# Two transformer blocks on one core: the opening by passes, top-k rounds paced by issued tiles, and a gate product between short latent products

## What is computed

```python
def reference(x, ...):
    x = first_block(x, ...)    # pooling, gated linear attention (GLA), forgetting attention (fox), feed-forward
    x = second_block(x, ...)
    return x

def second_block(x, ...):                                  # D = 1024, T = 512
    h = rmsnorm(x)
    (q_lat, c_kv, k_rope, z_a, q_b, k_b, v_b, z_b,
     q_idx, k_idx, w_idx, gate_a, gate_b) = split(h @ w_in)
    # latent attention (mla): 8 heads, queries from a latent of 384, keys and values from one of 256
    q = rmsnorm(q_lat) @ w_uq;   k, v_a = rmsnorm(c_kv) @ w_ukv       # rope on 32 of 96 features
    y_a = softmax(mask(q @ k)) @ v_a * silu(z_a)
    # sparse attention (dsa): 8 heads; an index score picks the keys of each query
    score = sum_heads(relu(q_idx @ k_idx) * w_idx);  idx = top_k(score, 128)
    y_b = softmax(q_b @ k_b[idx] + rel_bias) @ v_b[idx] * silu(z_b)
    x = x + (sigmoid(gate_a) * (y_a @ w_o_a) + sigmoid(gate_b) * (y_b @ w_o_b)) @ w_out
    return rmsnorm(x)
```

## Time and profile before

| | before |
|---|---|
| three runs | 1049.06, 1048.12, 1049.0 us; median 1049.0 |
| profiled execution | 1049.3 us, of which the span of its trace is 1047.5 us |
| mean granted clock of TensorE | 0.997 |
| busy: PE, PEld, DVE, ACT, POOL | 98%, 79%, 58%, 42%, 31% |
| matmuls | 5126 |
| dense tiles (form HH, WH of line 1454) | 800 matmuls, 403 ns each |
| moved by DMA | 102.39 MB, mean 98 GB/s |

### The profile page before, as it was taken

How to read it: one execution, slowest core, us unless ns; L and a number is a source line. 1 busy time by engine, 2 the same in 40 slices (tenths; PEclk the granted TensorE clock), 3 DMA queues, 4 the chain that set the end, 5 groups by cost and what they waited for, 6 DMA issues and landing times.

```text
span 1047.5 us, 13717 instructions
## 1 busy us (share of the span) xinstructions
PE 1030.2 (98%) x5126; PEld 832.4 (79%) x5126; DVE 603.8 (58%) x1087; ACT 443.9 (42%) x785; POOL 320.5 (31%) x374
## 2 busy tenths in 40 slices
PE   9999999999999999999999999989999999999997
PEld 7887877778888888888888878767887777788886
DVE  5875657575444432444457657888656666335544
ACT  6432656554232221233242346445755554323233
POOL 1344632440110000110113347333336666521101
PEclk9999999999999999999999999999999999999999
DMA  8222233123323322323322335211322323222312
GB/s 287 92 71 86 82 91 94 62 77 104 100 84 104 115 92 90 101 81 101 101 101 89 126 115 190 81 61 45 98 67 85 116 88 109 84 98 95 106 61 81
DMA packets 34898, 102.39 MB, mean 98 GB/s; under 512 B 4608, under 2 KB 8128, under 8 KB 34832
## 3 DMA queue, kind: packets, MB, share of 16 engines
q1 hardware_dynamic: 34560, 101.25, 29.7%
q10 hardware_dynamic: 272, 0.26, 0.1%
HBM read 93.40 MB, written 4.74 MB: 94 GB/s over the span
## 4 chain that ended last, share of the span: by engine, by line
PE 85%; DVE 8%; ACT 3%; issue 2%; DMA 1%; POOL 0%; SPq 0%; DVEq 0%; ACTq 0%; POOLq 0%
PE bank L1454 23%; PE bank L1458 23%; PE bank L1456 23%; PE bank L1586 3%; PE bank L1577 2%; PE bank L1477 1%; DVE score L2147 1%; PE bank L1478 1%; PE bank L1479 1%; DVE m L2145 1%; PE bank L1562 1%; DVE acc L1875 1%; ACT WH L1638 1%; DMA X<-xT 1%; PE bank L1496 1%
## 5 line engine op out<-in xcount | busy, mean ns | idle before, releaser
L1454 PE MATMUL bank<-HH,WH 128*128 128x512 f32 x800 | 322.7, 403 | 0.9 <-DVE HL L1866 0.6
L1458 PE MATMUL bank<-HH,WL 128*128 128x512 f32 x800 | 312.9, 391 | 0.0
L1456 PE MATMUL bank<-HL,WH 128*128 128x512 f32 x800 | 312.5, 391 | 0.0
L2234 POOL TENSOR_TENSOR WL<-WS,WH 128x256 fp32r<-128x256 f32 x256 | 203.5, 795 | 255.6 <-ACT WH L1638 239.6
L1638 ACT ACTIVATE WH<-WS 128x1024 fp32r<-128x1024 f32 x160 | 166.3, 1047 | 41.6 <-PE bank L1458 40.2
L1454 PEld LDWEIGHTS bank<-HH,WH 128*128 128x128 f32 x800 | 151.0, 189 | 38.5 <-issue 5.8
L1458 PEld LDWEIGHTS bank<-HH,WL 128*128 128x128 f32 x800 | 150.4, 188 | 32.3
L1456 PEld LDWEIGHTS bank<-HL,WH 128*128 128x128 f32 x800 | 150.9, 189 | 29.4 <-issue 1.4
L1856 DVE TENSOR_TENSOR WL<-WS,WH 128x1024 fp32r<-128x1024 f32 x96 | 125.1, 1308 | 30.8 <-ACT WH L1638 30.8
L2275 POOL TENSOR_TENSOR fa<-fa,fg 128x512 f32<-128x512 f32 x22 | 28.3, 1286 | 271.6 <-DVE fa L2087 271.6
L1454 PE MATMUL bank<-GH,WH 128*128 128x512 f32 x176 | 68.5, 389 | 0.0
(11 more groups left out here) (326 smaller groups left out, 1710.7 us busy)
## 6 DMA issues: line engine op xcount, KB each, us to landing
WS<-wall SPq DMA_DIRECT2D x161, 512.0 KB, 3.4
scratch<-rows SPq DMA_DIRECT2D x8, 320.0 KB, 5.4
X<-xT SPq DMA_DIRECT2D x8, 256.0 KB, 6.8
b_t<-scratch SPq DMA_DIRECT2D x8, 256.0 KB, 3.6
outT<-X SPq DMA_DIRECT2D x7, 256.0 KB, 2.3
b_m<-b_m SPq DMA_DIRECT2D x11, 128.0 KB, 2.3
f_s<-f_s SPq DMA_DIRECT2D x8, 128.0 KB
f_m<-f_m SPq DMA_DIRECT2D x8, 128.0 KB
```

Of the source, the lines that this page charges most:

```text
L1454: e.matmul(b[:, :], wh, xh[:, at_k, :], start=k == 0, stop=False)
L1456: e.matmul(b[:, :], wh, xl[:, at_k, :], start=False, stop=False)
L1458: m = e.matmul(b[:, :], wl, xh[:, at_k, :], start=False, stop=k == n - 1)
L2234: e.tensor_tensor(WL[:, u % NW, cs], WS[:, u % NST, cs], f32(WH[:, u % NW, cs]), ALU.subtract).then_inc(*tick(w_low_g, u if c == 3 else (u ...
```

## The change

It has four parts.

1. *Opening.* 10 fillers in place of 14. Chunk 0 of `X` is loaded by a DMA that ACT issues as its first instruction, and not by SP; SP's order after it is `V`, first half of unit 0, chunk 1, second half, chunk 2, unit 1, chunks 3 and 4, unit 2. ACT splits chunk 0 before the first half of unit 0. A new step `mm_firsts` has the three products of a chunk go together by passes: three times HH x WH, then three times HL x WH, then three times HH x WL, each with its own wait.
2. *Latent products.* `uq0` takes a bank of `t_ring`. The product `za1` no longer follows `uq3`; it comes ahead of `uk1`, that is between `uq1` and `uk1`.
3. *Pace of the top-k rounds.* `now["per"]` is 0 here. A wrapper `paced` around `attention` adds 0.25 for each yield of attention and 0.37 for each tile issued since (2 for a token-side product), and issues a round (or a step of `dsa_stack`) for each whole unit.
4. *Mixes.* `attention` yields once more ahead of each mix of latent attention, so that one more dense step lies there.

```diff
@@ the opening
-        do("split_first", half=0)
         for c in range(NK):
             do("halve_x", c=c)
             known.add(("h1", c))
-            if c == 0:
-                do("split_first", half=1)
+            if c < 2:
+                do("split_first", half=c)
                 unit_low[0], count["split"] = w_low_v, 1
...
-            for (name, _, _, _), (t, _), b in zip(firsts, tiles, early):
-                do("mm", name=name, tiles=[(t, k)], n=NK, x="h1", x0=0, b=b, free=None)
+            do("mm_firsts", names=[f[0] for f in firsts], tiles=[t for t, _ in tiles], k=k, b=early)
@@ attention
                         if to_c:
+                            if to_c[0]["a"] == "mla":
+                                yield
                             step_c()
@@ mla_products
-                                   + cols(96 * hd + 64, 16), "lq", 3, q_out(hd, hl))
-            if p:
+                                   + cols(96 * hd + 64, 16), "lq", 3, q_out(hd, hl),
+                                   ring=t_ring if hd == 0 else d_ring)
+            if p > 1:
                 yield from z_products("za", P_ZA, p)
@@ mla_side
+            yield from z_products("za", P_ZA, 1)
             yield from mla_products(1)
@@ the weave of the second block's attention
-        now["per"] = 1.5
+        def paced(main, per_tile, per_step):
+
+            due, seen = 0.0, len(steps)
+            for _ in main:
+                yield
+                due += per_step + per_tile * sum(len(s["tiles"]) if kind == "mm" else 2 * (kind == "mm_tok")
+                                                 for kind, s in steps[seen:])
+                seen = len(steps)
+                while due >= 1:
+                    due -= 1
+                    step_behind()
+
+        now["per"] = 0.0
...
+        weave(paced(attention(...), .37, .25), side, [0.9] * 66 + [0.85])
@@ SP
-                    for c in range(NK):
+                    for c in range(1, NK):
                         e.dma_start(X[:, c, :], xT[:, c, :]).then_inc(*x_in[c].tick())
-                        if c == 0:
+                        if c == 1:
                             e.dma_start(WS[:, 0, 512:1024], wall[0, :, 512:1024]).then_inc(*w_in[0].tick(0))
-                        elif c in (1, 3):
-                            load((c + 1) // 2)
+                        elif c in (2, 4):
+                            load(c // 2)
@@ TensorE
-                    for _ in range(14):
+                    for _ in range(10):
                         e.matmul(bank[2][:, 0:128], ones[:, :], ones[:, :], start=True, stop=True)
...
+                elif kind == "mm_firsts":
+
+                    k = s["k"]
+                    for t, b in zip(s["tiles"], s["b"]):
+                        q.wait_ge(hi(("h1", k)), w_hi("first" if t < 4 else t // UT))
+                        e.matmul(b[:, :], weights(t)[0], HH[:, k, :], start=k == 0, stop=False)
+                    for t, b in zip(s["tiles"], s["b"]):
+                        q.wait_ge(low(("h1", k)))
+                        e.matmul(b[:, :], weights(t)[0], HL[:, k, :], start=False, stop=False)
+                    for name, t, b in zip(s["names"], s["tiles"], s["b"]):
+                        q.wait_ge(w_low_v("first") if t < 4 else split_low(t // UT))
+                        m = e.matmul(b[:, :], weights(t)[1], HH[:, k, :], start=False, stop=k == NK - 1)
@@ ACT
                 if kind == "start":
+                    e.dma_start(X[:, 0, :], xT[:, 0, :]).then_inc(*x_in[0].tick())
                     e.preload_act_table_set(LN_EXP)
```

More of the change, by code:

```diff
@@ L1243, in build @@
             next(side)
-        weave(attention([(lambda p=p: p in mla_in and f"za{p}" in gates, lambda p=p: mla_pair(p)) for p in range(4)]
-                        + [(lambda p=p: dsa_ready(p), lambda p=p: dsa_pair(p))
-                           for p in range(4)],
-                        pc_ring, pt_ring), side, [0.9] * 66 + [0.85])
+        weave(paced(attention([(lambda p=p: p in mla_in and f"za{p}" in gates, lambda p=p: mla_pair(p)) for p in range(4)]
+                              + [(lambda p=p: dsa_ready(p), lambda p=p: dsa_pair(p))
+                                 for p in range(4)],
+                              pc_ring, pt_ring), .37, .25), side, [0.9] * 66 + [0.85])
         assert not behind and not first
@@ L1449, in tensor_program @@
                         wh, wl = weights(t)
-                        if t < 4:
-                            q.wait_ge(w_hi("first"), hi((s["x"], at_k)))
-                        else:
-                            q.wait_ge(s["free"] if k == 0 else None, split_low(t // UT), low((s["x"], at_k)))
+                        q.wait_ge(s["free"] if k == 0 else None, split_low(t // UT), low((s["x"], at_k)))
                         e.matmul(b[:, :], wh, xh[:, at_k, :], start=k == 0, stop=False)
-                        q.wait_ge(low((s["x"], at_k)))
                         e.matmul(b[:, :], wh, xl[:, at_k, :], start=False, stop=False)
-                        q.wait_ge(w_low_v("first"))
                         m = e.matmul(b[:, :], wl, xh[:, at_k, :], start=False, stop=k == n - 1)
                         ends = unit_ends([t], 1) + ([s["name"]] if k == n - 1 else [])
+                        if ends:
+                            m.then_inc(*dense.tick(*ends))
+                elif kind == "mm_firsts":
[9 more added lines that the diff above has]
+                        m = e.matmul(b[:, :], weights(t)[1], HH[:, k, :], start=False, stop=k == NK - 1)
+                        ends = unit_ends([t], 1) + ([name] if k == NK - 1 else [])
                         if ends:
```

## The result

The changed kernel takes 1042.34 us (median of 4 runs, 1042.17 to 1042.71) against 1048.78 us for the one before (4 runs, 1048.12 to 1049.06). The ratio is 0.9939, with a 95% interval of 0.9927 to 0.9950: 6.4 us or 0.6% faster, where 5.35 were forecast. The profiled execution took 1042.17 us with a span of 1040.2, that is 7.3 us less span than the profiled one before. In a later set of runs the same kernel had a median of 1042.85 beside 1049.09 for the one before.

The account below looks back on a forecast made before the run. TensorE, busy 98% of the span, was taken as the bound, so gains come where it waits or runs slowly. Opening -1.35 and latent attention -4.0 sum to -5.35: 1043.7 us against the 1049.0 median, range 1040.5 to 1047.0.

Parts of the forecast that it names:

- The reckoning of DVE: Latent attention: DVE's work counted from za1's last matmul at 667.3 puts (2,2)'s reciprocal at 708.5, its transpose at 709.2.
- The places of the new waits: Latent attention: new TensorE waits of 1.4 us at the transpose of (0,3), 2 at (2,2), the rest in pieces.
- the 3.7 that were taken back: Latent attention to (2,2): of 6.3 us gained, 3.7 come back as new waits for DVE, leaving 2.6 us.
- The added step: Ahead of each latent attention mix: takes the 0.4 us wait for `PT`, whose row leaves the wait list.
- The opening, -1.35: Start of kernel: first sum on `acc` at 21.2 in place of 22.55, all after it moves, -1.35 us.
- it is now unit 1 that lands at 10.0: Opening loads: with chunk 2 ahead of it on SP, weight unit 1 lands at 10.0, its high part ready at 11.05.
- Latent attention, -4.0: Index scores and latent attention: 2.6 us gained to the transpose of (2,2), 1.4 us behind it, together -4.0 us.
- The 0.6 us for DVE's `Pc`: TensorE's wait on `Pc` written by DVE, where the order is nearly the same: 0, and 0.6 either way.
- The half clock: TensorE at 1.2 GHz after the 2.73 us wait ending at 685.37: 1.7 us of clock lost, counted as regained.
- the clock takes it back: Rival, 0.20: clock falls at (2,2)'s wait and TensorE stays at 1.2 GHz in the opening, 1.7 us each; 1045.4 to 1047.
- It adds no matmul; it gives DVE time: za1 between uq1 and uk1: adds no matmul and gives DVE time to empty the banks of short products.
- The slower rival: Sparse attention, 0.05: postponed rounds late for its first mask, 1 us per uncovered round; eight late to end 2.1 above 1049.

Follow-up runs that it names:

- pace 0.50: Changed kernel with 0.50 top-k rounds for each tile in place of 0.37: 1051.32 us, ratio 1.0020 to the kernel before.
- pacing alone: Kernel before with only the pacing of the top-k rounds by issued tiles; uq0, za1, mixes and opening as before: 1044.53 us, ratio 0.9957.
- the opening alone: Kernel before with all of part 1 of the change, all else as before: 1047.17 us, ratio 0.9985.
- the order alone: Kernel before with only uq0 in a bank of t_ring and za1 ahead of uk1, pacing as before: 1048.71 us, ratio 0.9998.
- `za1` as before: Changed kernel with za1 back behind uq3, uq0 still in a bank of t_ring: 1043.07 us, ratio 0.9941 to the kernel before.
- 0.28: Changed kernel with 0.28 top-k rounds for each tile in place of 0.37: 1042.09 us, ratio 0.9932 to the kernel before.

## Why the prediction was right, and where its terms were off

**The reckoning of DVE held.** The prediction had `za1` taken from its bank at 667.3 on the clock of before; it was taken at 664.93, 2.4 us earlier, which is what the opening had gained. It put the reciprocal of (2,2) at 708.5; that came at 706.01, again 2.5 earlier. The transpose was to start at 709.2, and started at 706.88 + 2.4 = 709.3. So counting rounds ahead of a share, with 1.52 and 1.25 us for each, gave a point 41 us on to within 0.2 us. That it came so close is in part luck, since two errors nearly cancelled. The swish of `za1` was to wait for nothing, and waited 1.15 us in the changed kernel:

```profile
668.56 0.69 DVE L1920 SCALAR_TENSOR_TENSOR zb<-tmp,zb 128x512 f32<-128x512 f32 x1 [1.15 <-ACT tmp L1685]
```

And DVE's work was reckoned some 1.3 us too long (41.1 us less 1.85 of waits, so 39.2, where 40.5 were reckoned). 0.5 of that is a wait that the reading of DVE's idle time before left out:

```profile
698.38 1.41 DVE L2169 TENSOR_TENSOR a_k<-bank,RK 64x512 f32<-64x512 f32 x2 [0.49 <-PE bank L1458]
```

The run with pace 0.50 shows the same from the other side: four rounds more ahead of (2,2), and it is slower than before.

**The places of the new waits** were half wrong. 1.4 us was put at (0,3) and 2 at (2,2); there were 0.75 and 0.44. The rest stood at the bank of `uq2` (0.87), at (0,1) (0.33), for `a_q` (0.21) and at the first mix (0.72). Their sum, 3.3 us and a restart of 0.11 for each, is 4.0, the 3.7 that were taken back. In this case what TensorE paid followed from how late DVE was; who paid did not. Not all of the sum is DVE's lateness, though: the run with pacing alone, in which no transpose waits for `Pc`, has 0.73 us at the first mix too. There the prediction had a second miss. The added step was to take the 0.4 us for `PT`, and its row to be gone; it grew to 0.9.

**The opening, -1.35, was a term mis-sized.** The step that was off is "it is now unit 1 that lands at 10.0". Its split began at 8.9 here, and at 9.1 in the mean of the nine traces with passes and new loads; what was to follow it was right (11.25 us from the start of the split to the sum, where 1.05 + 9.8 + 0.35 = 11.2 were reckoned). So it was 2.4 us between the two profiled executions. But those two are the earliest and the latest sum on `acc` of the table, and that is luck: the two other traces with the opening of before have 22.14 and 21.87. The means, 22.2 for those three and 20.6 for the nine with passes and new loads, are 1.6 us apart, and the opening alone gave 1.8 in the medians. Against that the term was short by 0.3 to 0.5 us, not by 1.

**Latent attention, -4.0, was -4.9** (7.3 less the 2.4 of the opening), between these two traces, of which only the one before has the spell of half clock. Of the 6.4 us of the medians, 4.6 to 4.8 are left when 1.6 to 1.8 are taken off for the opening. To the transpose of (2,2) 2.5 us of this had come, where 2.6 were forecast. The 0.6 us for DVE's `Pc`, put at 0 with 0.6 either way, went as well, and with it the second `Pc` wait, the one for `acc` and their restarts; the row of DVE's `Pc` is not in the list after.

**The half clock** was counted as 1.7 us of gain. The run of the opening alone shows an execution without it, with the wait left at 2.68 us, and there DVE took 0.9 of 1.6 us back. Waits of 2.26 and 2.43 us in two other traces left the clock alone too, so it came in one of four traces with a wait of over 2.2 us.

The other executions have no trace, but their mean granted clock is on record. The 13 traces without a spell have 0.997 or 0.998 (the clock is low in their last 3 to 6 us, at the program's end), and a spell of 1.7 us lost takes 0.0016 off. So a mean of 0.996 or less points to at least one spell, while 0.997 can be either; the profiled execution before has 0.997. It came in 13 of 45 executions of the kernel before, and in 4 of 11, 5 of 11 and 2 of 5 of the opening alone, the order alone and `za1` as before, the three others with a wait over 2.2 us. It also came in 4 of 11 with pace 0.50, whose waits are up to 1.8 us but many. In the other nine rows (the changed kernel twice, and seven variants of it or of pacing alone) it came in none of 44. So the kernels that waited longest are the ones in which the clock fell, though in under half of their executions. The price in the medians was small: for the kernel before 1049.2 us at 0.996 or less against 1048.9 at 0.998 (only `za1` as before shows more, 1044.6 against 1041.8, in five executions). The 1.7 us were a reading of one execution, and little of them can be in the 6.4.

The rival *the clock takes it back* did not come behind a wait. Its other half did, in small: in four traces by passes the first dense matmuls ran at the lower rate, and the first three took 0.4 to 0.7 us longer.

**"It adds no matmul; it gives DVE time"** was the sentence on za1, and it was wrong in what it suggests. The sum took the order as a gain of 1.2 us (1.09 and a restart). By the runs, the order alone gives nothing and within the change it costs 0.6 to 0.9 us. DVE finds no round to do while `za1` runs, as the prediction said itself, and is behind from there. That fits the waits, but the run with `za1` put back alone does not prove it: the bank of `uq0` by itself brought a wait of 2.43 us.

**The slower rival** (rounds late for the masks) did not come at 0.37, where the last round begins 12 us earlier than before. With 0.28 there are two small waits in sparse attention, 1.12 and 0.90 us; whether it begins there stays open.

## What to carry to other kernels

When work of one engine is dealt between steps of another, its pace is worth tuning against what the other engine issues: here 0.37 rounds for each tile gave 4.5 us by itself, 0.28 is as good within the change, and with 0.50 the whole change is 2.2 us slower than none. Whether counting tiles beats a lower rate for each call was not tried. To forecast such a change, count what stands ahead of the waited-for instruction in its engine's queue and add durations; trust the sum more than the places of the waits. And a wait that is removed by giving one product another bank can come back at the next, as it did here, when the engine that empties the banks is late: look for idle time of that engine ahead of it instead.

## What the runs showed of the hardware

TensorE's step from the lower to the higher rate at the start came at another time in each execution: 28 filler passes took 5.98 us before and 5.36 with 14 fillers in the changed kernel. The column PEclk doesn't show it (it has 1.00 from 4 to 5 us in both), only the spacing of the passes does. And the same wait, 2.73 and 2.68 us at the same transpose, was followed by a granted clock of 0.66 in one execution and 1.00 in the other. Over all executions a mean granted clock of 0.996 or less came in 28 of 83 of the five kernels with the longest waits or the most of them, and in none of 44 of the others.
